# Stick-breaking attention with a running softplus sum on GpSimd, sums of squares as two rounded products, and a new order in its fourth steps and its last head pair

## The reference

```python
o = rms_norm(o, o_norm_g) * jax.nn.silu(gate)
```

```python
q = rms_norm(q.reshape(Bn, T, SB_HEADS, SB_DH), q_norm_g)
k = rms_norm(k.reshape(Bn, T, SB_HEADS, SB_DH), k_norm_g)
z = jnp.einsum('bqhd,bshd->bhqs', q_blk, k) * scale
mask = key_pos[None, :] < q_pos[:, None]
log1m = jnp.where(mask, -jax.nn.softplus(z), 0.0)
after = lax.cumsum(log1m, axis=3, reverse=True) - log1m
wts = jnp.where(mask, jnp.exp(jax.nn.log_sigmoid(z) + after), 0.0)
o = jnp.einsum('bqhs,bshd->bqhd', wts, v)
```

## Time and profile before

| | us |
|---|---|
| median of 3 runs | 1822.09 (1820.61 to 1824.07) |
| the profiled execution | 1820.88 |
| its span, first to last instruction | 1819.1 |
| mean granted PE clock | 0.998 of 2.4 GHz |

### The profile page before, as it was taken

One profiled execution on the slowest core, in us unless ns is written; L12 is line 12 of the kernel. 1 busy time (PEld: TensorE's weight loads), 2 busy tenths in 40 slices (PEclk: granted clock), 3 DMA queues, 4 the chain that ended last, 5 costly groups with the idle time before them and its releaser, 6 DMA issues.

```text
span 1819.1 us, 22598 instructions
## 1 busy us (share of the span) xinstructions
PE 1767.8 (97%) x8872; PEld 1431.8 (79%) x8872; DVE 851.8 (47%) x1294; ACT 824.9 (45%) x1191; POOL 550.3 (30%) x143
## 2 busy tenths in 40 slices
PE   7999999999999999999999999999999999999999
PEld 5688789878898666668878888888877887887787
DVE  6765954242142555544643444441277577434410
ACT  6575343685233666644422222222266734338721
POOL 1333320333424000024344444444334234104443
PEclk9999999999999999999999999999999999999999
DMA  4223210222222010112223222222222132012222
GB/s 171 93 70 93 77 39 17 78 93 93 93 93 93 24 47 27 44 47 96 90 94 104 101 92 92 92 98 96 96 84 81 69 102 74 12 47 93 92 94 69
DMA packets 48775, 143.69 MB, mean 79 GB/s; under 512 B 28080, under 2 KB 30256, under 8 KB 32816
## 3 DMA queue, kind: packets, MB, share of 16 engines
q1 hardware_dynamic: 48688, 142.50, 22.9%
HBM read 137.25 MB, written 5.24 MB: 78 GB/s over the span
## 4 chain that ended last, share of the span: by engine, by line
PE 71%; issue 17%; POOL 4%; DVE 4%; ACT 4%; DMA 0%; POOLq 0%; SPq 0%; DVEq 0%; ACTq 0%
PE ps L1565 18%; PE ps L1567 18%; PE ps L1566 18%; POOL w_lo L441 4%; PE ps L1828 2%; PE ps L1884 2%; PE ps L1855 1%; PE ps L2030 1%; PE ps L1870 1%; PE ps L1879 1%; PE ps L2045 1%; PE ps L1839 1%; PE ps L2003 1%; ACT w_hi L531 1%; PE ps L1950 1%
## 5 line engine op out<-in xcount | busy, mean ns | idle before, releaser
L441 POOL TENSOR_TENSOR w_lo<-w_raw,w_hi 128x2048 fp32r<-128x2048 f32 x107 | 497.2, 4646 | 1054.1 <-ACT w_hi L531 842.1
L1565 PE MATMUL ps<-h_hi,w_hi 128*128 128x512 f32 x1488 | 604.3, 406 | 21.8 <-DVE w_lo L959 10.0
L1567 PE MATMUL ps<-h_hi,w_lo 128*128 128x512 f32 x1488 | 581.7, 391 | 0.0
L1566 PE MATMUL ps<-h_lo,w_hi 128*128 128x512 f32 x1488 | 581.3, 391 | 0.0
L1565 PEld LDWEIGHTS ps<-h_hi,w_hi 128*128 128x128 f32 x1488 | 280.4, 188 | 105.0 <-issue 28.9
L1566 PEld LDWEIGHTS ps<-h_lo,w_hi 128*128 128x128 f32 x1488 | 280.6, 189 | 59.5 <-issue 5.5
L1567 PEld LDWEIGHTS ps<-h_hi,w_lo 128*128 128x128 f32 x1488 | 280.2, 188 | 59.6
L531 ACT ACTIVATE w_hi<-w_raw 128x2048 fp32r<-128x2048 f32 (+1 forms) x126 | 238.7, 1894 | 129.1 <-PE ps L1567 123.8
L1565 PE MATMUL ps<-y_hi,w_hi 128*128 128x512 f32 x448 | 174.3, 389 | 0.0
L1566 PE MATMUL ps<-y_lo,w_hi 128*128 128x512 f32 x448 | 174.3, 389 | 0.0
L1567 PE MATMUL ps<-y_hi,w_lo 128*128 128x512 f32 x448 | 174.3, 389 | 0.0
(11 more groups left out here) (190 smaller groups left out, 2285.7 us busy)
## 6 DMA issues: line engine op xcount, KB each, us to landing
w_raw<-w_tiles SPq DMA_DIRECT2D x124, 1024.0 KB, 4.9
x<-x_t SPq DMA_DIRECT2D x4, 512.0 KB, 6.8
out_t<-x SPq DMA_DIRECT2D x8, 256.0 KB, 5.7
w_raw<-w_tiles SPq DMA_DIRECT2D x2, 512.0 KB, 5.0
scr_u<-lt SPq DMA_DIRECT2D x8, 128.0 KB, 2.7
u_blk<-scr_u SPq DMA_DIRECT2D x2, 512.0 KB, 3.3
scr_v<-v_blk SPq DMA_DIRECT2D x2, 512.0 KB, 2.6
scr_t<-v_t SPq DMA_DIRECT2D x2, 512.0 KB, 3.6
```

The lines of the kernel that those rows point to most:

```text
L441: pool.tensor_tensor(w_lo[:, slot, :], w_raw[:, slot, :], w_hi[:, slot, :].bitcast(F32), ALU.subtract).then_inc(lo_done, 1)
L1565: pe.matmul(out_, w_h, m_h, start=start, stop=False)
L1566: pe.matmul(out_, w_h, m_l, start=False, stop=False)
L1567: return pe.matmul(out_, w_l, m_h, start=False, stop=stop)
```

## The change

Four things change.

1. **Running sum.** POOL adds up the softplus of all later key blocks (`run`), and rounds it into `run_hi` and `run_lo`. From v = 2 on, `cum` multiplies that sum once by the matrix of ones in place of each block apart.
2. **Squares.** ACT writes the squares rounded (`sq_hi`); POOL squares again in float32 (`sb_sq`) and subtracts (`sq_lo`); PE sums both parts with a rounded matrix. In DeltaNet, DVE splits the summed squares into `ns_hi` and `ns_lo`, and PE does two rounded matmuls.
3. **Fourth steps.** `sums(j+1, 1)` stands right behind `z` of step 3, ACT's `rms_qk` between Abs and Exp of that step, its `square_qk` ahead of the softplus of step 2, DVE's `scaled_qk` ahead of the softplus of step 3.
4. **Last pair and start.** The eight blocks left for the last pair are spread two per step; half of gate tile t0+13 (`early_half(0)`) stands ahead of the last `cum`, the other half behind the last `pv`. At the start, 5 and 3 blocks stand behind the first two `sums` in place of 8 behind both.

The core of the diff:

```diff
+        def running(j, v):
+            n = 4 * j + 2 * (v - 1)
+            off = (0, 128, 384)[v]
+            head = slice(3 * P - P * (v + 1), 3 * P - P * v)
+            rest = slice(3 * P - P * v, 3 * P)
+            whole = slice(3 * P - P * (v + 1), 3 * P)
+            own = slice(0, 2 * P) if v == 1 else slice(2 * P, 5 * P)
+            pool.wait_ge(b["sp"], 2 * (4 * j + v) + 2)
+            pool.tensor_copy(run[:, :, head], sb_sp[:, :, off:off + P]).then_inc(b["run"], 1)
+            before = sb_sp[:, :, 0:P] if v == 1 else run[:, :, rest]
+            pool.tensor_tensor(run[:, :, rest], sb_sp[:, :, off + P:off + P * (v + 1)], before, ALU.add).then_inc(b["run"], 1)
+            pool.wait_ge(b["run"], n + 2)
+            pool.tensor_copy(run_hi[:, :, own], run[:, :, whole]).then_inc(b["runh"], 1)
+            pool.wait_ge(b["runh"], 2 * j + v)
+            pool.tensor_tensor(run_lo[:, :, own], run[:, :, whole], run_hi[:, :, own].bitcast(F32), ALU.subtract)\
+                .then_inc(b["runl"], 1)
+        def square_low(p, c):
+            n = 2 * p + c
+            pool.wait_ge(b["raw"], n + 1)
+            ...
+            pool.tensor_tensor(sb_sq[:, :], sb_raw[:, c, :], sb_raw[:, c, :], ALU.mult).then_inc(b["sqf"], 1)
+            pool.wait_ge(b["sqf"], n + 1)
+            pool.wait_ge(b["sq"], n + 1)
+            ...
+            pool.tensor_tensor(sq_lo[:, c, :], sb_sq[:, :], sq_hi[:, c, :].bitcast(F32), ALU.subtract).then_inc(b["sql"], 1)
...
+                for j in range(SB_PAIRS):
+                    if j + 1 < SB_PAIRS:
+                        square_low(j + 1, 0)
+                    running(j, 1)
+                    if j + 1 < SB_PAIRS:
+                        square_low(j + 1, 1)
+                    running(j, 2)
...
+                dve.tensor_copy(ns_hi[:, :], nsq[:, 0, :]).then_inc(nhi_done, 1)
+                dve.wait_ge(nhi_done, n + 1)
+                dve.tensor_tensor(ns_lo[:, :], nsq[:, 0, :], ns_hi[:, :].bitcast(F32), ALU.subtract).then_inc(nlo_done, 1)
...
-                pe.matmul(ps[4][:, :], ones, nsq[:, 0, :], start=True, stop=True).then_inc(nss_done, 1)
+                pe.matmul(ps[4][:, :], ones_r[:, :], ns_hi[:, :], start=True, stop=False)
+                pe.matmul(ps[4][:, :], ones_r[:, :], ns_lo[:, :], start=False, stop=True).then_inc(nss_done, 1)
...
-                pe.matmul(ps[c][:, :], cf[:, C_BLOCK:C_BLOCK + P], sb_sq[:, c, :], start=True, stop=True).then_inc(b["ss"], 1)
+                pe.wait_ge(b["sql"], 2 * p + c + 1)
+                pe.matmul(ps[c][:, :], block_r[:, :], sq_hi[:, c, :], start=True, stop=False)
+                pe.matmul(ps[c][:, :], block_r[:, :], sq_lo[:, c, :], start=False, stop=True).then_inc(b["ss"], 1)
...
             fill(16)
             sums(0, 0)
+            fill(5)
             sums(0, 1)
-            fill(8)
+            fill(3)
             for j in range(SB_PAIRS):
                 more = j + 1 < SB_PAIRS
                 for v in range(4):
                     g = 4 * j + v
                     z(g)
-                    fill(2)
-                    if more and v in (1, 3):
-                        sums(j + 1, v // 2)
+                    if more and v == 3:
+                        sums(j + 1, 1)
+                    fill(2 if more else 1)
+                    if more and v == 1:
+                        sums(j + 1, 0)
                     if g >= 2:
                         pv(g - 2)
-                    fill(1)
+                    fill(1 if more else 0)
                     if g:
                         cum(g - 1)
                     fill(1)
             last = 4 * SB_PAIRS - 1
             pv(last - 1)
+            early_half(0)
             cum(last)
             pv(last)
```

More of the change, by code:

```diff
@@ L196, in trunk @@
     tri_r = sb("tri_r", [P, 2 * P], F32R, offset=big_at + (8 * T + 4608) * 4)
+    run_at = big_at + (8 * T + 4864) * 4
+    run = sb("run", [P, 2, 3 * P], offset=run_at)
+    run_hi = sb("run_hi", [P, 2, 5 * P], F32R, offset=run_at + 6 * P * 4)
+    run_lo = sb("run_lo", [P, 2, 5 * P], F32R, offset=run_at + 16 * P * 4)
     arena = at[0]
@@ L324, in trunk @@
     zeroed = sem("rows_zeroed")
+    rounded = sem("consts_rounded")
     tap_done = sem("conv_tap")
@@ L340, in trunk @@
     b = {n: sem("sb_" + n) for n in
-         "gq8 tri vev sq raw ss r qk v z abs exp ln1 sp sph spl cum w pv ev gate".split()}
+         "gq8 tri vev sq raw ss r qk v z abs exp ln1 sp sph spl cum w pv ev gate sqf sql run runh runl".split()}
     c_ = {n: sem("sc_" + n) for n in "zero c cu cstep conv y gate".split()}
@@ L437, in _ @@
         pool.memset(row_parts[:, :, :], 0.0).then_inc(zeroed, 1)
+        pool.wait_ge(loaded, 32)
+        pool.tensor_copy(ones_r[:, :], ones).then_inc(rounded, 1)
+        pool.tensor_copy(block_r[:, :], cf[:, C_BLOCK:C_BLOCK + P]).then_inc(rounded, 1)
         def low(t, i, slot):
@@ L806, in square_qk @@
                     act.wait_ge(b["ss"], 2 * p + c - 1)
-                act.activation(sb_sq[:, c, :], sb_raw[:, c, :], ACT.Square).then_inc(b["sq"], 1)
+                act.activation(sq_hi[:, c, :], sb_raw[:, c, :], ACT.Square).then_inc(b["sq"], 1)
             def rms_qk(p, c):
@@ L853, in stickbreak @@
                     g = 4 * j + v
[L854 to L858 removed]
+                    if more and v == 2:
+                        square_qk(j + 1, 1)
+                    softplus(g, j + 1 if more and v == 3 else None)
+                    if more and v == 0:
+                        square_qk(j + 1, 0)
+                    if more and v == 1:
+                        rms_qk(j + 1, 0)
                     if g:
                         weights(g - 1)
[L861 removed]
+                    if v == (2 if more else 3):
                         hi(t0 + 7 + j)
@@ L1462, in stickbreak @@
                         low_w(t0 + 6 + j)
-                    if more and v in (1, 3):
-                        scaled_qk(j + 1, v // 2)
+                    if more and v == 1:
+                        scaled_qk(j + 1, 0)
                     if v == 2 and j:
@@ L2020, in cum @@
                         pe.wait_ge(b["spl"], 6 * j + 2 * (v - 1) + e + 1)
-                    for v2 in range(v, -1, -1):
-                        w2 = P * (v2 + 1)
-                        off = (0, 128, 384, 768)[v2]
-                        c = 0 if v2 == v else P
-                        if v2 == 0:
-                            mm = pe.matmul(bk[:, w - w2:w], cf[:, C_TRI + c:C_TRI + c + P], sb_sp[:, e, 0:w2],
+                    if v:
+                        off = (0, 128, 384, 768)[v]
+                        for part in (sp_hi, sp_lo):
+                            mm = pe.matmul(bk[:, 0:w], tri_r[:, 0:P], part[:, e, off - P:off - P + w],
+                                           start=False, stop=(v > 1 and part is sp_lo), skip_group_check=True)
+                    if v < 2:
+                        mm = pe.matmul(bk[:, w - P:w], cf[:, C_TRI + P * v:C_TRI + P * v + P], sb_sp[:, e, 0:P],
+                                       start=False, stop=True, skip_group_check=True)
+                    else:
+                        if e == 0:
+                            pe.wait_ge(b["runl"], 2 * j + v - 1)
+                        own = slice(0, 2 * P) if v == 2 else slice(2 * P, 5 * P)
+                        for part in (run_hi, run_lo):
+                            mm = pe.matmul(bk[:, P:w], tri_r[:, P:2 * P], part[:, e, own],
                                            start=False, stop=True, skip_group_check=True)
-                            continue
-                        for part in (sp_hi, sp_lo):
-                            pe.matmul(bk[:, w - w2:w], tri_r[:, c:c + P], part[:, e, off - P:off - P + w2],
-                                      start=False, stop=False, skip_group_check=True)
                     mm.then_inc(b["cum"], 1)
@@ L2077, in stickbreak, with early_half @@
             pv(last - 1)
+            def early_half(c):
+                if c == 0:
+                    ready(t0 + 13)
+                for k in range(KD):
+                    mm = in_block(t0 + 13, c, k)
+                mm.then_inc(proj_done, 1)
+            early_half(0)
             cum(last)
@@ L2081, in gate_step @@
             def gate_step(t, i, k):
-                if k:
+                if k == 1 and isinstance(i, int):
+                    early_half(1)
+                elif k:
                     in_tile(t, i)
```

43 lines of the change are left out of this document (31 added, 12 removed).

## The result

The changed kernel took 1790.78 us (median of 4 runs, 1787.89 to 1792.42), the kernel before beside it 1822.94 (4 runs): ratio 0.9828, 95% interval 0.9817 to 0.9839, some 32 us less. The profiled execution took 1792.42 us with a span of 1790.6, so 28.5 us less than the profiled execution of before (its mean clock, 0.997, is the lowest of the four, and its time the longest; hence 28.5 and not 32).

A forecast was written before the change was run, and what follows sets the result against it. PE, busy for 97% of the span, was taken as the bound. Terms -6.6 + 0.75 - 1.15 - 10.8 - 4.5 = -22.3 us gave a likeliest median of 1799.8 us, with an 8-in-10 range of 1791 to 1812.

The forecast's parts named there:

- DeltaNet, both layers: Gate tiles: two rounded passes replace each float32 sum, 0.41 us saved per head in 2 layers of 8, 6.6 us.
- start of the pairs: Before the first scores: the second sums stands behind five blocks, so sb_qk comes late, +0.75 us.
- six steady pairs: Stick-breaking stage: each steady pair 1.8 us shorter, to 25.4 us, -10.8 us for six.
- last pair, t0+13: Last pair and the gate tile behind it: 38.8 us becomes 33.8; 4.5 us taken because PE keeps a hole.
- Step 2: Third step of a pair: POOL holds up DVE, sb_raw comes 1.25 us late, the step grows by 0.75 us.
- Step 0: First step of a pair: cheaper cum saves 0.92 us, late squares and softplus cost 0.25, together -0.65 us.
- Step 1: Second step of a pair: the cheaper sum of squares on the path saves 0.4 us.
- Step 3: Fourth step of a pair: early sb_qk and cheaper sums save 1.5 us off 8.53; ACT then carries it.
- (B): Pairs: POOL holds the port for all four running operations, step 2 grows by 2.3 us; 1810.7 us, chance 0.17.
- (C): Pairs: POOL's lock and dearer copies also delay step 3, slower than before, near +17, 1839 us; chance 0.05.
- (D): Pairs: freed time becomes wait for ACT's weights; only DeltaNet and last pair pay, -11, 1811 us; chance 0.10.
- (A): Pairs: the port is free in effect, POOL's passes fall into DVE's holes; -29.6, 1792.5 us, chance 0.20.

The follow-up runs named there:

- the kernel without the running sum: The changed kernel with POOL's running sum removed, so cum multiplies each later block again: 1798.56 us, ratio 0.9875 to the kernel before.
- the order alone: The kernel before with only the new order of the fourth steps and of the square: 1814.65 us, ratio 0.996.
- the two profiles above: Profiles of the changed kernel without POOL's running sum (1798.56 us) and with an added 1024-column POOL pass (1795.71 us).
- the 512-column pass: The changed kernel with one more unused POOL pass of 512 columns ahead of each v = 1 running sum: 1790.65 us.

## Why the prediction was right, and where it was not

The kernel became faster, and DeltaNet, steps 3 and 0 of the pairs, and the last pair are where it did, as forecast. The size is less well met than one number suggests: the pairs gave 8.5 us more than forecast and the start 2.75 less, and these misses of opposite sign made up for each other in part. That is luck. By its own terms, between the two profiled executions:

| term | forecast | measured |
|---|---|---|
| DeltaNet, both layers | -6.6 | -6.3 |
| start of the pairs | +0.75 | +3.5 |
| first pair | -1.15 | -1.7 |
| six steady pairs | -10.8 | -18.7 |
| last pair, t0+13 | -4.5 | -5.2 |
| sum | -22.3 | -28.4 (spans: -28.5) |

- **DeltaNet** was right: -3.4 us up to `sb_raw` (the start of the stage comes 2.6 to 3.6 us earlier over the profiles with this change), and -2.9 in what lies behind tile t0+13 (1009.0 us then, 1006.1 now).
- **Step 2, the term that failed.** It had +0.75 us, for a `sb_raw` 1.25 us late; measured 0 in six pairs, for 0.07 late, and +0.33 in the first. "If step 2 stays at 5.4" stands in the prediction as a sign of being wrong in mechanism, and it came. Three things were wrong. I counted two DVE operations as standing behind a whole POOL pass each; they alternate with POOL's, and a wait is only what is left of the one pass that runs. I let the delay add to DVE's queue, where a hole of 0.41 us took most of it. And ACT had 0.9 us to spare, not 0.5: by the table above a `sb_raw` 1.25 us late would have cost 0.3. The earlier trace rows show one long pass against one operation; they give no price for short ones in turn. This is 6 x 0.75 + 0.42 = 4.9 us, the largest single miss.
- **Step 0** was -0.65 (-0.92 and 0.25 make -0.67) and is -0.94: PE's part (0.92) was met, 0.97 by the kernel without the running sum; the 0.25 us for late squares and softplus did not come.
- **Step 1** was -0.4 and is -0.37.
- **Step 3** was -1.5 and is -1.84. The hole's share (1.15) is 1.10 by the order alone. I let ACT's row of operations cap the rest; the products gave 0.34 (running sum) and 0.28 (squares) more, since PE was idle for only 0.10 us of the pair; 0.12 us is left over.
- **The last pair** was close. The 1.6 us hole kept in step 3 did not come as such: there are three waits for ACT's weights, 1.4 us together, and the clock stays up.
- **The start** was mis-sized by 2.75 us, and all of it is clock. That blocks stand behind Ln as before was right (576.77, before 580.18 and DeltaNet 3.4 earlier). At full clock the scores would follow the hole by 6.28 us, as in the two profiles above, so at 583.05: 0.6 us late, where the forecast had 0.75. But two float32 sums of 0.87 us used to fill this time, with holes of 1.84 us in all in the stretch 570 to 585; one sum of 0.46 leaves 3.35 in one piece, and in this profile the clock then falls. I had priced blocks at 0.69 us there; they took 1.3. A lower clock behind the hole was no term of the sum.
- **Of the rivals,** (B) is refuted by the 512-column pass, (C) by step 2, (D) by PE's 0.10 us of idle time. (A) was met in every step of a steady pair, but not in its reason: POOL's passes do not fall into DVE's holes. They meet DVE in every pair, and what is left of the meeting is taken up by a hole of DVE's and by ACT's spare time. Its sum (-29.6) missed the loss at the start.

What stays open: why the clock falls behind the same hole of 3.35 us in six of eight profiles and not in two. The program up to the hole is the same in all eight.

## What to carry to other kernels

Remove the hole first, then the work: the cheaper products were worth nothing in the pairs while PE waited for a norm, and nearly their full price once it did not. When a shared way is feared, lay the passes beside each other one by one, and look for the hole in the victim's queue: what matters is the remainder of one pass less that hole, and less what the next engine in the chain has to spare. Where work ahead of a wait gets cheaper, look at what the wait becomes, since a longer hole on PE can bring the lower clock with it, though it does not in every execution.
